# Raw rows into the output projection and the feed-forward part, with the norm factors at the evictions, and throwaway matmuls in the routing

## The reference, cut to what matters

```python
# first block
mixed = concat([rms_norm(attn_out, g_out[:512]),      # 512 columns
                rms_norm(conv_out, g_out[512:])])     # 512 columns
x = x + mixed @ w_o
h = rms_norm(x, g_ffn_norm)
x = x + square(relu(h @ w_up)) @ w_down
...
# second block, its mixture of experts (32 experts, each token uses 2)
h = modulate(rms_norm(x, norm2_g), shift2, scale2)
grp, top_e = argmax of group, top 2 of its 8 experts
x = x + gate2 * sum over the chosen experts of weight * expert(h)
return rms_norm(x, final_norm_g)
```

## Time and profile before

| what | value |
|---|---|
| median of three runs | 1686.05 us (1681.72 to 1686.2) |
| the profiled execution | 1685.19 us |
| its span in the profile | 1683.2 us |
| PE busy | 1513.2 us (90%) |
| DVE, ACT, POOL busy | 768.4, 456.2, 588.5 us |
| mean granted TensorE clock | 0.947 of 2.4 GHz |

### The profile page before, as it was taken

The page is one execution under the profiler, slowest core; times in us unless marked ns, Lnnn a source line. Parts: engine busy times, 40 slices in busy tenths (PEclk is TensorE's granted clock), DMA queues, the critical chain, the costliest instruction groups (busy, mean ns, idle before and its releaser), DMA issues.

```text
span 1683.2 us, 21076 instructions
## 1 busy us (share of the span) xinstructions
PE 1513.2 (90%) x8288; PEld 1201.1 (71%) x8288; DVE 768.4 (46%) x1466; ACT 456.2 (27%) x716; POOL 588.5 (35%) x477
## 2 busy tenths in 40 slices
PE   6878999889999999979999989999999959977882
PEld 5877787768888888857888978785588846544441
DVE  2343756448677774244513730255413254433234
ACT  4233234333231322242323332343223121000001
POOL 2482121235445544523533224421144313222222
PEclk9978999899999999989999989999999979998896
DMA  5231010033544452222322112220043559999994
GB/s 226 76 105 72 26 51 26 26 125 150 210 177 179 186 200 99 78 80 97 110 76 100 51 50 100 79 82 26 2 174 150 241 224 366 377 396 379 397 373 161
DMA packets 36914, 256.70 MB, mean 153 GB/s; under 512 B 7232, under 2 KB 7872, under 8 KB 13008
## 3 DMA queue, kind: packets, MB, share of 16 engines
q1 hardware_dynamic: 31056, 246.94, 38.5%
q0 software_dynamic: 5760, 8.41, 1.5%
HBM read 250.59 MB, written 15.20 MB: 158 GB/s over the span
## 4 chain that ended last, share of the span: by engine, by line
PE 82%; DVE 8%; issue 4%; ACT 4%; POOL 1%; DMA 1%; SPq 0%; DVEq 0%; POOLq 0%; ACTq 0%
PE G L1976 13%; PE G L1977 13%; PE G L1978 13%; PE SA L2496 4%; PE G L2496 4%; PE SA L1976 3%; PE SA L1978 3%; PE SA L1977 3%; PE PB L1976 3%; PE PB L1978 3%; PE PB L1977 3%; PE OB L2160 2%; PE G L2018 2%; PE PB L2504 1%; PE SA L2391 1%
## 5 line engine op out<-in xcount | busy, mean ns | idle before, releaser
L710 POOL TENSOR_TENSOR wl<-raw,wh 128x512 fp32r<-128x512 f32 x364 | 488.4, 1374 | 718.7 <-ACT wh L837 709.0
L837 ACT ACTIVATE wh<-raw 128x2048 fp32r<-128x2048 f32 x91 | 174.2, 1915 | 298.0 <-PE SA L1978 153.7
L1976 PE MATMUL G<-Hh,wh 128*128 128x512 f32 x544 | 218.0, 401 | 4.9 <-DVE arena L1440 1.7
L1977 PE MATMUL G<-Hl,wh 128*128 128x512 f32 x544 | 214.3, 394 | 0.0
L1978 PE MATMUL G<-Hh,wl 128*128 128x512 f32 x544 | 214.2, 394 | 0.0
L1513 DVE SCALAR_TENSOR_TENSOR arena<-arena,st 128x256 f32<-128x256 f32 x144 | 136.0, 945 | 5.1
L1976 PEld LDWEIGHTS G<-Hh,wh 128*128 128x128 f32 x544 | 103.8, 191 | 26.1 <-issue 2.1
L1978 PEld LDWEIGHTS G<-Hh,wl 128*128 128x128 f32 x544 | 103.5, 190 | 22.7
L1977 PEld LDWEIGHTS G<-Hl,wh 128*128 128x128 f32 x544 | 103.8, 191 | 19.9
L2018 PE MATMUL G<-con,arena 128*128 128x128 f32 x264 | 47.0, 333 | 43.2 <-ACT arena L853 26.9
L779 POOL DMA_INDIRECT raw<-xn_rows,arena x38 | 36.9, 971 | 133.0 <-PE G L2512 106.9
(11 more groups left out here) (472 smaller groups left out, 3096.9 us busy)
## 6 DMA issues: line engine op xcount, KB each, us to landing
raw<-in_pieces_dram SPq DMA_DIRECT2D x91, 1024.0 KB, 4.8
arena<-in_pieces_dram SPq DMA_DIRECT2D x24, 1024.0 KB, 4.8
arena<-in_wexp_dram SPq DMA_DIRECT2D x11, 2048.0 KB, 39.5
dn_w<-in_wexp_dram SPq DMA_DIRECT2D x22, 1024.0 KB, 35.7
arena<-in_wexp_dram SPq DMA_DIRECT2D x12, 1024.0 KB, 34.8
gu_y<-in_wexp_dram SPq DMA_DIRECT2D x6, 2048.0 KB, 37.8
gu_h<-in_wexp_dram SPq DMA_DIRECT2D x6, 2048.0 KB, 33.8
gu_l<-in_wexp_dram SPq DMA_DIRECT2D x6, 2048.0 KB, 34.9
```

Source lines behind the costliest of these rows:

```text
L710: ins = pool.tensor_tensor(low_[:, part], whole[:, part], high[:, part], ALU.subtract)
L837: act.activation(wh[:, split_slot(s)], wait_raw(act, sp_list[s]), ACT.Copy).then_inc(S("high_split"), 1)
L1976: pe.matmul(out, ah, bh, start=first, stop=False)
L1977: pe.matmul(out, ah, bl, start=False, stop=False)
```

## The change

Two parts.

1. *The end of the first block.* PE turns the raw attention rows (`Oat`) and, after the projection, the raw rows of `x` (`Xv`). The row factors are applied later: the attention's when DVE evicts the projection's attention half, and that of the row norm, squared, when DVE evicts the `down` matmuls, since relu and square of a row scaled by r are those of the raw row times r*r. The two scalings in between are removed (four instructions on DVE for the attention rows, two on ACT and two on DVE for the rows of `x`). The column sums `csq` move on PE from ahead of the transposes to between projection pieces 0 and 1, on DVE their copy to behind the first four evictions; the square of the last row tile moves behind the low parts of `h1`; POOL makes three more low parts (pieces 20 to 22) before the row factor.
2. *The routing.* `hold(n)` issues n matmuls of 256 columns whose result nothing reads: 10 before the counting, 7 before the placing, 5 before the first `rows_of`, 3 between the second `rows_of` and the first expert.

On SP the load of the first modulation piece waits for `ss_attn` (ACT's squares of the attention rows) too, and two waits on `rows_normed` count one step of `NT` less; these lines are left out below.

```diff
@@ -143,9 +143,10 @@
         g += [(w, i, "v") for w, i in CMP_STEPS.get(4 * n, ())]
         i, k = divmod(n, 6)
         g += [(("hc", "cg", "bg")[k // 2], 2 * i + k % 2, "a" if k < 2 else "v")]
+    g += [("aT", f, "v") for f in range(4)]
+    g += [("wo", i, "v") for i in range(4)]
     g += [("csq", 0, "v")]
-    g += [("aT", f, "v") for f in range(4)]
-    g += [("wo", i, "v") for i in range(16)]
+    g += [("wo", i, "v") for i in range(4, 16)]
     g += [("h1", f, "v") for f in range(KT)]
     m = 0
     for r in range(FQ):
...
@@ -746,11 +748,13 @@
             rstd_of(rqk[:, 4:8], msqk[:, 4:8], ssqk[:, 4:8], NT, 512).then_inc(S("rstd_conv"), 1)
             for p in sp_list[16:20]:
                 low(p)
+            for p in sp_list[20:23]:
+                low(p)
             pool.wait_ge(S("ss_x"), 2)
             pool.wait_ge(S("ss_last"), 2)
             rstd_of(rstd, ms, ss, NT, D).then_inc(S("rstd_x"), 1)
             NB1 = len(first_pieces()) + len(ffn_pieces())
-            for p in sp_list[20:NB1]:
+            for p in sp_list[23:NB1]:
                 low(p)
             pool.wait_ge(S("ss_x"), 3)
             pool.wait_ge(S("ss_last"), 3)
@@ -962,7 +966,6 @@
             high(18)
             high(19)
             squares(1, hraw, ss, [("wo", 13), ("wo", 14)])
-            norm_rows(1, hraw, rstd)
             transposed_high("h1", KT, Hhv, cols(par, PAR, "g_ffn"))
             s = 20
             for r in range(FQ):
@@ -1466,29 +1469,27 @@
                 dve.wait_ge(S("conv_high"), f + 1)
                 dve.scalar_tensor_tensor(Ylv[:, 4 + f, :], conv[:, f, :], go[:, 4 + f:5 + f], Yhv[:, 4 + f, :].bitcast(F32),
                                          ALU.mult, ALU.subtract).then_inc(S("conv_low"), 1)
-            b = wait_group(dve, "csq", 0)
-            free_group(dve.tensor_copy(ssqk[:, 4:8], b[:, 0:4]), "csq", 0)
+            transposed_low("aT", 4, Ylv, Yhv, go)
+
             dve.wait_ge(S("rstd_attn"), 1)
-            for t in range(NT):
-                dve.tensor_scalar(kT[:, t, :], Oat[:, t, :], rqk[:, t:t + 1], None, ALU.mult).then_inc(S("attn_normed"), 1)
-            transposed_low("aT", 4, Ylv, Yhv, go)
-
-            dve.wait_ge(S("rstd_conv"), 1)
             for half in range(2):
                 for t in range(NT):
                     i = 8 * half + t
                     xt = Xv[:, t, half * 512:(half + 1) * 512]
                     b = wait_group(dve, "wo", i)
-                    free_group(dve.tensor_tensor(xt, xt, b[:, :], ALU.add), "wo", i)
+                    free_group(dve.scalar_tensor_tensor(xt, b[:, :], rqk[:, t:t + 1], xt, ALU.mult, ALU.add), "wo", i)
+                if half == 0:
+                    b = wait_group(dve, "csq", 0)
+                    free_group(dve.tensor_copy(ssqk[:, 4:8], b[:, 0:4]), "csq", 0)
+                    dve.wait_ge(S("rstd_conv"), 1)
                 for t in range(NT):
                     i = 8 * half + 4 + t
                     xt = Xv[:, t, half * 512:(half + 1) * 512]
                     wait_freed(dve, "wo", i - 4)
                     b = wait_group(dve, "wo", i)
                     free_group(dve.scalar_tensor_tensor(xt, b[:, :], rqk[:, 4 + t:5 + t], xt, ALU.mult, ALU.add), "wo", i)
+            transposed_low("h1", KT, Hlv, Hhv, cols(par, PAR, "g_ffn"))
             square_last(hraw, ss, "wo", 15)
-            norm_rows(1, hraw, rstd)
-            transposed_low("h1", KT, Hlv, Hhv, cols(par, PAR, "g_ffn"))
             m = 0
 
             def mod_cols(m):
@@ -1530,11 +1531,14 @@
                     if m < MOD_PIECES:
                         mod_part(m)
                     half = j // 2
+                    if r == j == 0:
+                        dve.wait_ge(S("rstd_x"), 2)
+                        own(dve.tensor_tensor(ms, rstd, rstd, ALU.mult))
                     for t in range(NT if j % 2 else 0):
                         i = (r * 2 + half) * 4 + t
                         xt = Xv[:, t, half * 512:(half + 1) * 512]
                         b = wait_group(dve, "down", i)
-                        free_group(dve.tensor_tensor(xt, xt, b[:, :], ALU.add), "down", i)
+                        free_group(dve.scalar_tensor_tensor(xt, b[:, :], ms[:, t:t + 1], xt, ALU.mult, ALU.add), "down", i)
                     if m < MOD_PIECES:
                         mod_cols(m)
                         m += 1
@@ -2190,23 +2194,23 @@
                 if 0 <= t - 2 < len(units):
                     values(t - 2)
 
-            bank = group("csq", 0)
-            pe.wait_ge(S("conv_sq"), 4)
-            for t in range(NT):
-                for f in range(4):
-                    ins = pe.matmul(bank[:, t:t + 1], SPsq(f)[:, t * P:(t + 1) * P], one, start=f == 0, stop=f == 3)
-            filled(ins)
-            pe.wait_ge(S("attn_normed"), NT)
+            pe.wait_ge(S("attn_sum"), 2 * NT)
             for f in range(4):
-                transposes("aT", f, [kT[:, t, f * P:(f + 1) * P] for t in range(NT)])
+                transposes("aT", f, [Oat[:, t, f * P:(f + 1) * P] for t in range(NT)])
             wait_freed(pe, "aT", 3)
             for n in range(4):
                 if n == 1:
+                    bank = group("csq", 0)
+                    pe.wait_ge(S("conv_sq"), 4)
+                    for t in range(NT):
+                        for f in range(4):
+                            ins = pe.matmul(bank[:, t:t + 1], SPsq(f)[:, t * P:(t + 1) * P], one, start=f == 0, stop=f == 3)
+                    filled(ins)
                     pe.wait_ge(S("conv_low"), 4)
                 wide_rows("wo", ("wo", n), 4 * n, n % 2, act=(Yhv, Ylv), whole=True)
-            pe.wait_ge(S("rows_normed"), 2 * NT)
+            wait_freed(pe, "wo", 15)
             for f in range(KT):
-                transposes("h1", f, [hraw[:, t, f * P:(f + 1) * P] for t in range(NT)])
+                transposes("h1", f, [Xv[:, t, f * P:(f + 1) * P] for t in range(NT)])
 
             def mod_piece(m):
                 bank = group("mod", m)
@@ -2237,7 +2241,7 @@
                         m += 1
 
 
-            pe.wait_ge(S("rows_normed"), 3 * NT)
+            pe.wait_ge(S("rows_normed"), 2 * NT)
             for f in range(KT):
                 transposes("h2", f, [hraw2[:, t, f * P:(f + 1) * P] for t in range(NT)])
             pe.wait_ge(S("sml_done"), 2)
@@ -2461,6 +2465,11 @@
                 dst = (bank, SA[0])[t // 2]
                 ins = pe.transpose(dst[:, t * 36:(t + 1) * 36], gr_rows[r, (t % 2) * P:(t % 2 + 1) * P], ident[r, r])
             filled(ins)
+            def hold(n):
+                for _ in range(n):
+                    pe.matmul(SA[1][:, 0:256], ident, con[:, 0:256], start=True, stop=True)
+
+            hold(10)
             pe.wait_ge(S("assigned"), 1)
             bank = group("cnt", 0)
             for t in range(NT):
@@ -2477,6 +2486,7 @@
             pe.matmul(bank[0:32, 32:33], tri[0:32, 0:32], nbc[0:32, :], start=True, stop=True)
             ins = pe.matmul(bank[:, 33:34], one[0:32, :].to_broadcast([32, P]), nbc[0:32, :], start=True, stop=True)
             filled(ins)
+            hold(7)
             pe.wait_ge(S("places_ready"), 1)
             bank = group("slots", 0)
             for c in range(8):
@@ -2546,8 +2556,10 @@
 
                 return pe.matmul(out, src, idn, start=True, stop=True)
 
+            hold(5)
             rows_of(0)
             rows_of(1)
+            hold(3)
             for b in range(NE):
                 pe.wait_ge(S("xgT_ready"), b + 1)
                 pe.wait_ge(S(f"gu_loaded{b % NSLOT}"), slot_count(b))
```

More of the change, by code:

```diff
@@ L603, in _ @@
                     if p[1] == 0:
+                        sp.wait_ge(S("ss_attn"), 1)
                         wait_group(sp, "wo", 0)
@@ L622, in _ @@
                 if p == ("om", 0):
-                    sp.wait_ge(S("rows_normed"), 3 * NT)
+                    sp.wait_ge(S("rows_normed"), 2 * NT)
                     sp.dma_start(x_spill, X[:, :]).then_inc(S("x_spilled"), 16)
@@ L656, in _ @@
             expert_gu(4)
-            sp.wait_ge(S("rows_normed"), 4 * NT)
+            sp.wait_ge(S("rows_normed"), 3 * NT)
             sp.dma_start(xn_rows.rearrange("(t p) n -> p t n", p=P), xn).then_inc(S("xn_stored"), 16)
```

## The result

The changed kernel takes 1690.21 us (median of 6 runs, 1689.23 to 1691.93) against 1684.81 us (6 runs, 1681.72 to 1686.20) of the kernel before: ratio 1.0036, 95% interval 1.0025 to 1.0047. The profiled execution took 1690.46 us, its span is 1688.5 us. The chain that ended last reads as in the earlier trace rows, 82% PE, so the account can again be made by asking when PE starts its next dense piece.

The account below looks back on a forecast made before the run. TensorE, 82% of the chain that ended last, was taken as the bound, so edits count by when PE starts its next dense piece. Projection 9.7 - feed-forward 5.3 - routing 3.5 = +0.9 us, so 1686.1 us; range 1681.5 to 1691.

Parts of the forecast that it names:

- The projection: Output projection after the first attention: it ends 9.7 us later (7.2 to 11.2), 12.4 lost less 2.7 gained.
- start: Start of the output projection: raw attention rows let it begin 2.7 us sooner, at about 315.4.
- from the sums to piece 1: Ahead of projection piece 1: PE waits 1.8 us for copy and factor, then 5.0 for POOL's low part.
- restart at half clock: Projection piece 1: after standing 6.8 us PE restarts at half clock, costing 2.0 us (1.4 to 2.2).
- Rival 2: Projection: the wait ahead of piece 1 is hidden, so 8.8 us go, giving 1677.3; chance 0.08.
- The feed-forward start: Between projection and feed-forward part: transposes needn't wait for scaled rows, a gain of 5.3 us (4.7 to 5.5).
- the cover of 1.5 us: First modulation sum: ready 1.5 us before PE used it, so DVE's 1.3 us delay costs nothing, up to 0.2 uncovered.
- rival 4: Feed-forward start: transposes don't hold the clock, so it starts at 1.2 GHz, 2.0 us, giving 1688; chance 0.05.
- The routing: Routing up to the first expert: throwaways keep PE at full clock, a gain of 3.5 us (1.5 to 4.3).
- The term for the last three: Ahead of the first expert's matmuls: three throwaways stand on the path and cost 1.3 us.
- Rival 1: Routing: throwaways run at half clock, first expert starts 6.6 us later, +11 in all, 1696; chance 0.07.
- Rival 3: Expert stage: full DMA queues keep the routing's 3.5 us gain from arriving, giving 1689.6; chance 0.08.

Follow-up runs that it names:

- ffn_only: The kernel before with only the feed-forward half of the change (raw rows of x, squared factor at the down evictions): 1678.14 us, ratio 0.9960.
- throwaways_only: The kernel before with all 25 throwaway matmuls and nothing else of the change: 1680.58 us, ratio 0.9975.
- after_again: The changed kernel, unaltered, measured once more for a second profile: 1691.27 us, ratio 1.0044.
- low_first: The changed kernel with POOL making projection piece 1's low part before it waits for the column sums: 1681.33 us, ratio 0.9982.
- csq_back: The changed kernel with the column sums and their copy back at their old place, ahead of the attention's transposes: 1677.74 us, ratio 0.9960.
- csq_back_no_three: The changed kernel with the column sums back at their old place and without the last three throwaways: 1674.92 us, ratio 0.9946.
- longer_throwaways: The kernel of csq_back_no_three with 12, 12 and 7 throwaways instead of 10, 7 and 5: 1675.50 us, ratio 0.9944.
- after: The changed kernel itself against the kernel before, in its first measurement and profile: 1690.21 us, ratio 1.0036.
- after_third: The changed kernel, unaltered, in a single further execution for a third profile: 1688.37 us.
- no_last_three: The changed kernel without the three throwaways between the second tokens' transposes and the first expert's matmuls: 1688.51 us, ratio 1.0026.

## Why the prediction was right in its range and 4 to 5 us short

**The projection.** The mechanism is as forecast, and each term was measured: start -2.8 (forecast -2.7), sums 3.63 (3.6), from the sums to piece 1 6.56 (1.8 + 5.0), restart at half clock from 339.22 to about 343.6 (0.70 in its window), 2.2 (2.0). The end moved by 374.31 - 363.81 - 1.2 of the attention sum's own delay = 9.3 us in the pair of profiles. These add up to 9.6; the other 0.3 is piece 0, which took 12.5 us to the start of what follows it, instead of 12.8. Rival 2, the hidden wait, is refuted. What was off is the reference: the first profile of before contains a restart at half clock in piece 0, which the other two of before lack (63.6 against 61.2 and 61.4). Against the mean of the three, 62.1, the loss is 10.8 us, 1.1 more than forecast. Of the two further kernels that have the old projection, ffn_only shows 63.6 us and throwaways_only 61.2, so the restart stands in two executions of five. The stated bounds of this term, 7.2 to 11.2, don't follow from the bounds of its parts, which add up to 8.7 and 11.7 and would have put the range at about 1683 to 1691.7; the result lies in both ranges.

**The feed-forward start.** The transposes start 0.81 us after the last eviction's start, as worked out, and the first high part 0.69 us after them instead of 1.15 (forecast 0.4 less). The prediction misread the pace behind it. It took 2.46/3 = 0.82 us for DVE's own; but one low part takes 0.75 us in both kernels, and before, ACT's high parts had waited 0.17 us each for PE's transposes, which ran at half clock until 373.12. In the changed kernel the clock is full there and three low parts take 2.07 us (from 376.60). So the gain was 12.53 - 6.75 = 5.8 us in the profiles' pair, 5.9 by the means, not 5.3. The row sum on DVE behind the low parts left the first modulation sum ready at 391.64 + 0.48 = 392.12, and PE took it at 392.27: the cover of 1.5 us is used up, and 0.2 was paid (0.44 us from the start of the matmul before it, where the kernel before had 0.23). (By the earlier trace rows the clock was lost at about 366.3, not 366.7; nothing hangs on it.) The Trainium skill ("TensorE: Matmul & The Clock Gate", Part 4) says that a transpose doesn't count as PE activity in the same way; here the grant is 1.00 in 378 to 379, in a stretch of transposes alone, so rival 4 is refuted as far as this stretch goes.

**The routing, the failed step.** "PE enters the first gap at full clock. If it stays" was the condition, and I gave it too much weight. It entered at full clock and didn't stay: the grant fell at about 1371.0, after ten throwaways that ended at 1368.9, 1.53 us of idle time and light matmuls. Of the 3.5 us the three profiles show 0.5, 4.1 and 1.5 (mean 2.0, each against the mean of before), and the medians show none (1690.26 us without the throwaways, 1690.21 with them). The profiled executions of the changed kernel lie on the fast side of its runs, so the mean of three is rather too kind. Where the clock falls only once in the routing, the gain is there: in those six profiles of kernels with throwaways (after_again, low_first, csq_back, throwaways_only, csq_back_no_three, longer_throwaways) the second expert starts 31.5 to 32.8 us after the logits, and in the three where it falls twice (after, after_third, no_last_three) 33.7 to 34.9. The term for the last three, 1.3, fits: without them the median is 1.7 us lower, within overlapping intervals. Rival 1 was half right: seven throwaways at half clock, but not the ten; the first expert starts 29.56 us after the logits against 29.51, not 6.6 us later. Rival 3 has nothing for it: from the second expert to the end it is 293.85 us after and 293.77 before; over all profiles it varies from 291.9 to 294.8, and the mean of the six early ones, 293.0, is no longer than that of the rest, 293.4.

**What was not forecast.** The later projection at 1217.74 starts at half clock, on the same 1.64 us of idle time after the same transposes with which the kernel before kept 1.00. Before, its first matmul took 0.50 us, not 0.80:

```profile
1213.34 0.50 PE L1976 MATMUL G<-Hh,wh 128*128 128x512 f32 x1 [1.64 <-DVE Yl L1744]
```

It costs 1.4 us. The middle adds 0.3 and the attention 0.4, within what executions of one kernel differ by.

By the means, then: 0.4 + 10.8 - 5.9 + 0.3 + 1.4 - 2.0 = +5.0 us, which is the difference of the means of the three profiled executions (1688.63 - 1683.59). The ratio says +6.1 (and +7.4 in the second batch, 1.0044); a routing gain of 1 instead of 2 us would bring the sum to +6.0, but no profile shows that. Of the 4.1 us between the forecast's +0.9 and +5.0, 1.1 lie in the projection's reference, 1.5 in the routing, 1.4 in the later projection, 0.7 in middle and attention, less 0.6 in the feed-forward start.

**What stays open.** The throwaways gained 4.2 us on the kernel before and nothing on the changed one. The profiles show that the moment at which the grant falls differs, even between executions of one program (5.34 and 3.29 us for the same seven), and that most of the gain in the routing goes with it. What sets that moment wasn't found. The same holds for the later projection: 150.9 us in all profiles of before and in ffn_only, 152.3 to 152.5 in all others, throwaways_only too, whose edits all lie behind that projection in the program.

## What to carry to other kernels

When a row factor moves to an eviction, look at what computes it and at what that engine has queued behind it: here a reduction moved in between two dense pieces, and the in-order engine that waited for its result also owed the next piece's operand, which cost more than the whole change gained. One line that makes the operand first removed the wait, and leaving the reduction where it was gave the rest. A gain in start time is worth little where it moves dense work into a stretch at half clock: here 1.7 us of earlier start left 0.3 to 0.5 us (csq_back against two executions of before). The gain of throwaway matmuls is to be taken from several executions and by medians, since one profile can show all of their gain or none.

## What the runs showed of the hardware

- The grant fell behind one-column matmuls though the record shows PE without a pause: in low_first 32 of them take 3.63 us, between dense pieces, and the grant fell just ahead of 334, 1.0 us after their end, with 512-column matmuls already running.
- The same instructions with the same idle time keep the clock in one execution and lose it in the next (seven throwaways in 3.29 or 5.34 us; the start of piece 0 at half clock in one of three executions of the kernel before).
- While POOL's low parts run (1.27 us an instruction), tiny DVE instructions on SBUF take as long as one of them: 1.29 us at 383.65 for 8 columns, and 1.22 and 1.34 for the two that follow, where the same three took 0.16, 0.17 and 0.35 us with POOL idle in the kernel before. The third of them has 256 columns.
